# A Fourier mixer over half of the token frequencies, mirrored by a sum and a difference

## What is computed

```python
FOURIER_GROUPS = 4
def fourier_mixer(x, w_out):
    B, S, D = x.shape
    xg = x.astype(jnp.float32).reshape(B, S, FOURIER_GROUPS, D // FOURIER_GROUPS)
    y = jnp.fft.fft2(xg, axes=(1, 3), norm='ortho').real.reshape(B, S, D)
    return y.astype(x.dtype) @ w_out
...
        x = layer_norm(DEEPNORM_ALPHA * x + mix, ln1_gain[layer], ln1_bias[layer])
        ffn = hierarchical_moe_2(x, router_coarse_w[layer], router_coarse_b[layer], router_fine_w[layer],
                               router_fine_b[layer], expert_w_gate[layer], expert_w_up[layer],
                               expert_w_down[layer])
        x = layer_norm(DEEPNORM_ALPHA * x + ffn, ln2_gain[layer], ln2_bias[layer])
```

## Time and profile before

| | us |
|---|---|
| median of 3 runs | 2004.66 |
| lowest and highest run | 2002.22, 2005.18 |
| profiled execution | 2002.44 |
| its span | 2000.5 |
| its mean granted TensorE clock | 0.951 of full |
| Fourier stage in it, first matmul to the first of the next stage | 1451.55 to 1482.64 |

### The profile page before, as it was taken

How to read it: one execution, slowest core, us unless ns; L and a number is a source line. 1 busy time by engine, 2 the same in 40 slices (tenths; PEclk the granted TensorE clock), 3 DMA queues, 4 the chain that set the end, 5 groups by cost and what they waited for, 6 DMA issues and landing times. The chain is left out here.

```text
span 2000.5 us, 20692 instructions
## 1 busy us (share of the span) xinstructions
PE 1785.5 (89%) x8544; PEld 952.9 (48%) x8544; DVE 674.3 (34%) x1347; ACT 427.7 (21%) x713; POOL 83.4 (4%) x66
## 2 busy tenths in 40 slices
PE   7999897895799999799799999899597999998995
PEld 6884454695455555456434443333254344442331
DVE  3657333446223334443412222122303122221223
ACT  2321224352222221222211111111112111111110
POOL 0000001311100000120100000000001000000000
PEclk9999998797899999899799999999897999999998
DMA  5345320004669996432999999999793999999995
GB/s 194 127 162 178 123 88 4 0 1 194 243 249 398 403 419 266 144 155 73 384 423 423 423 423 423 423 424 423 299 375 143 424 423 423 423 423 424 423 423 232
DMA packets 100017, 581.49 MB, mean 291 GB/s; under 512 B 23947, under 2 KB 26251, under 8 KB 34893
## 3 DMA queue, kind: packets, MB, share of 16 engines
q1 hardware_dynamic: 87997, 577.81, 70.8%
q10 hardware_dynamic: 11920, 2.26, 0.6%
HBM read 577.39 MB, written 2.62 MB: 290 GB/s over the span
## 5 line engine op out<-in xcount | busy, mean ns | idle before, releaser
L1717 PE MATMUL up_ps_l<-pool,hT 128*64 128x512 f32 x640 | 143.5, 597 | 13.4 <-DMA pool<-in_expert_w_up 13.4
L1717 PE MATMUL gate_ps_l<-pool,hT 128*64 128x512 f32 x640 | 141.4, 593 | 6.6 <-DMA pool<-in_expert_w_gate 5.3
L446 PE MATMUL proj_ps<-pool,hT 128*128 128x512 f32 x320 | 140.2, 598 | 5.6 <-DVE pool L684 5.6
L1740 PE MATMUL y_ps_l<-pool,hidden_l 128*64 128x512 f32 x640 | 142.6, 596 | 2.3 <-ACT hidden_l L1803 1.4
L1870 DVE SCALAR_TENSOR_TENSOR y_low_l<-y_ps_l,slot_gate_l,y_high_l 128x512 fp32r<-128x512 f32 x64 | 47.1, 751 | 251.2 <-ACT y_high_l L1813 251.2
L438 PE MATMUL proj_ps<-hT,pool 128*128 128x256 f32 x512 | 111.9, 380 | 0.0
L1860 DVE TENSOR_TENSOR hidden_l<-hidden_l,up_ps_l 128x512 f32<-128x512 f32 x32 | 22.0, 688 | 245.2 <-PE up_ps_l L1717 245.2
L438 PEld LDWEIGHTS proj_ps<-hT,pool 128*128 128x128 f32 x512 | 96.9, 190 | 14.8 <-issue 1.8
L446 PEld LDWEIGHTS proj_ps<-pool,hT 128*128 128x128 f32 x320 | 61.4, 192 | 81.3 <-issue 74.7
L1717 PEld LDWEIGHTS gate_ps_l<-pool,hT 128*64 128x64 f32 x640 | 45.5, 137 | 98.4 <-issue 87.6
L1717 PEld LDWEIGHTS up_ps_l<-pool,hT 128*64 128x64 f32 x640 | 43.6, 137 | 99.4 <-issue 77.8
(11 more groups left out here) (503 smaller groups left out, 2682.0 us busy)
## 6 DMA issues: line engine op xcount, KB each, us to landing
pool<-in_expert_w_gate SPq DMA_DIRECT2D x40, 2048.0 KB, 32.4
pool<-in_expert_w_up SPq DMA_DIRECT2D x40, 2048.0 KB, 30.2
pool<-in_expert_w_down SPq DMA_DIRECT2D x40, 2048.0 KB, 32.1
pool<-in_w_in_blocks SPq DMA_DIRECT2D x18, 2048.0 KB, 7.7
pool<-in_moe_w_gate SPq DMA_DIRECT2D x12, 2048.0 KB, 12.6
pool<-in_moe_w_up SPq DMA_DIRECT2D x12, 2048.0 KB, 12.0
pool<-in_moe_w_down SPq DMA_DIRECT2D x12, 2048.0 KB, 11.6
gate_room<-in_expert_w_gate SPq DMA_DIRECT2D x12, 2048.0 KB, 29.9
```

The source lines that it names most:

```text
L446: last = mm(pp[:, n % 2, j * W:(j + 1) * W], k.hT[:, c, j * P:(j + 1) * P], wbuf[n % 2][:, c, :], start=(c == 0), stop=(c == KC - 1))
L1717: last = mm(out[e * CAP:(e + 1) * CAP, 0:H], xg(part * r + c)[:, at:at + CAP], ex.weights(i, e, c), start=(part + c == 0), stop=(part == e ...
L1740: last = mm(Y[e * CAP:(e + 1) * CAP, n], hidT[:, part * r + c, e * CAP:(e + 1) * CAP], ex.weights(i, e, c)[:, n * W:(n + 1) * W], start=(p ...
```

## The change

The table now has three parts of 256 columns for each token half: cosines of frequencies 0 to 128 beside sines of 1 to 127, then all cosines, then all sines, 768 KB in place of 512 KB. The first product takes only the first part, so its matmuls are 256 columns wide and not 512. The second keeps the cosine and the sine contributions apart: for each output chunk two matmuls of 129 columns sum the cosine part and two of 127 columns the sine part, into neighbouring columns of one bank. ScalarE copies once per chunk after the first product (L2479 and L2480 become one) and once after the second, now to a region `uv` with the scale 1/T. VectorE gets three instructions for each chunk: the difference u - v is token frequencies 1 to 127, the sum u + v is frequencies 255 down to 129, written in mirrored order, and frequencies 0 and 128 are copied.

```diff
--- before.py
+++ after.py
@@ -98,8 +98,9 @@
 
     t = np.arange(T)
     ang = 2 * np.pi * ((t[:, None] * t[None, :]) % T) / T
-    both = np.stack([np.cos(ang), np.sin(ang)], 1).astype(np.float32)
-    return np.ascontiguousarray(both.reshape(NJ, P, 2, T).transpose(1, 0, 2, 3))
+    c, s = np.cos(ang), np.sin(ang)
+    rows = np.concatenate([c[:, 0:P + 1], s[:, 1:P], c, s], 1).astype(np.float32)
+    return np.ascontiguousarray(rows.reshape(NJ, P, 3 * T).transpose(1, 0, 2))
 
 
 ROPE_N = 2 * (64 + 32) * NJ
@@ -2441,13 +2442,16 @@
 
 def stage_fourier(k, ahead):
 
     nc = k.nc
-    s_a, s_ao, s_b = (k.sem(f"dft_{n}") for n in ("rows_product", "rows_out", "columns_product"))
+    s_a, s_ao, s_b, s_bo = (k.sem(f"dft_{n}") for n in ("rows_product", "rows_out", "columns_product", "columns_out"))
     scope = ExitStack()
     k.scope = scope
     with scope:
-        a = k.carve(k.gate_room, CHUNK, [P, KC, 2, T])
+        a = k.carve(k.gate_room, CHUNK, [P, KC, T])
+        uv = k.carve(k.gate_room, CHUNK + KC * T, [P, KC, T])
         ps = [k.ps(f"dft_ps{b}", [P, 2, T]) for b in range(8)]
+        cos, sin = slice(0, P + 1), slice(P + 1, T)
         with nc.Block() as block:
             @block.sync
             def _(sp):
@@ -2455,32 +2459,40 @@
 
             @block.tensor
             def _(pe):
+                mm = nc.tensor.matmul
                 pe.wait_ge(k.s_dft, 16)
                 for c in range(KC):
                     for j in range(NJ):
-                        last = nc.tensor.matmul(ps[c][:], k.x[:, j, c * P:(c + 1) * P], k.dft[:, j],
-                                                start=(j == 0), stop=(j == NJ - 1))
+                        last = mm(ps[c][:, 0], k.x[:, j, c * P:(c + 1) * P], k.dft[:, j, 0:T],
+                                  start=(j == 0), stop=(j == NJ - 1))
                     last.then_inc(s_a, 1)
                 for g in range(KC // 2):
-                    pe.wait_ge(s_ao, 4 * (g + 1))
+                    pe.wait_ge(s_ao, 2 * (g + 1))
                     for o in range(2):
-                        n = 0
-                        for f in range(2):
+                        for f, part in ((1, cos), (2, sin)):
                             for q in range(2):
-                                last = nc.tensor.matmul(ps[2 * g + o][:, 0, :], k.dft[:, q, f, o * P:(o + 1) * P],
-                                                        a[:, 2 * g + q, f, :], start=(n == 0), stop=(n == 3))
-                                n += 1
+                                last = mm(ps[2 * g + o][:, 0, part], k.dft[:, q, f * T + o * P:f * T + (o + 1) * P],
+                                          a[:, 2 * g + q, part], start=(q == 0), stop=(q == 1))
                         last.then_inc(s_b, 1)
 
             @block.scalar
             def _(act):
                 for c in range(KC):
                     act.wait_ge(s_a, c + 1)
-                    nc.scalar.activation(a[:, c, 0], ps[c][:, 0], ACT.Copy).then_inc(s_ao, 1)
-                    nc.scalar.activation(a[:, c, 1], ps[c][:, 1], ACT.Copy, scale=-1.0).then_inc(s_ao, 1)
+                    nc.scalar.activation(a[:, c], ps[c][:, 0], ACT.Copy).then_inc(s_ao, 1)
                 for c in range(KC):
                     act.wait_ge(s_b, c + 1)
-                    nc.scalar.activation(k.hT[:, c, :], ps[c][:, 0], ACT.Copy, scale=1.0 / T)
+                    nc.scalar.activation(uv[:, c], ps[c][:, 0], ACT.Copy, scale=1.0 / T).then_inc(s_bo, 1)
+
+            @block.vector
+            def _(dve):
+                tt = nc.vector.tensor_tensor
+                for c in range(KC):
+                    dve.wait_ge(s_bo, c + 1)
+                    u, v = uv[:, c, 1:P], uv[:, c, sin]
+                    tt(k.hT[:, c, 1:P], u, v, ALU.subtract)
+                    tt(k.hT[:, c, T - 1:P:-1], u, v, ALU.add)
+                    nc.vector.tensor_copy(k.hT[:, c, 0:T:P], uv[:, c, 0:P + 1:P])
     k.scope = k.ctx
 
 
@@ -2557,7 +2569,7 @@
             k.ctx = k.scope = outer
         k.gate_room = k.sb("gate_room", [P, 2 * CHUNK])
         split_rows("l")
-        k.dft = k.carve(k.gate_room, 0, [P, NJ, 2, T])
+        k.dft = k.carve(k.gate_room, 0, [P, NJ, 3 * T])
         for n in range(2):
             ex[1 + n].ring(k.gate_room, 2)
             ex[1 + n].ring(k.store, 2)
```

## The result

The changed kernel takes **1990.72 us** (median of 4 runs, 1989.95 to 1991.04), the kernel before, in runs on the same chip, 2004.45 (4 runs, 2002.22 to 2005.18): a ratio of 0.9933, 95% interval 0.9916 to 0.995. That is 13.7 us less by the medians. What of this scatter belongs to the change is a question in itself, taken up after the rows.

The account below looks back on a forecast made before the run. TensorE was taken to bound the Fourier stage, which lies on the path to the first expert and its train of transfers. -13.5 + 0.7 + 0.7 = -12.1 us, put on the median 2004.66: 1992.5 us, range 1989 to 1995.5, with rivals (a) and (b) 1988.8 to 1997.5.

Parts of the forecast that it names:

- The train: Expert-weight transfers from the first expert to the end, 418 us at 421 GB/s, claimed to move as a whole.
- The case in which transfers eat the gain: Rival: weights bound the kernel from 1442 to the end, so a shorter stage only lengthens a wait; 2004.7 us, chance 0.04.
- The rest: DMA standstill ahead of the first expert, ring full: 21 us by which the last loads could land later at no cost.
- the rule that each us is worth 0.5: First product: each us the clock rises earlier or later than 5.2 us after the start changes the saving by 0.5 us.
- +-0.8: First product: allowance in us around the 6.9 us saving for when the clock rises.
- rival (a): Second product: odd widths or the offset of 129 are slow on TensorE; 1995.8 or 1999.2 us, chance 0.09.
- Tail: End of the Fourier stage: VectorE's work on the last chunk lies on the path, +0.7 us.
- rival (b): Second product: VectorE becomes the bound, with a slow mirrored sum; +3.5 us, 1996.0 us, chance 0.05.
- The late bias: Norm after the Fourier stage: `bias_l` lands behind expert chunks, making `turn(0)` wait about +0.7 us (0 to 2.8).
- the landing: Arrival of `bias_l` for the norm after the Fourier stage, forecast at about 1488.4 (1487.3 to 1490.6).
- rival (d): Fourier stage and output product: shorter matmuls leave the clock low, making the kernel slower, up to 2023 us; chance 0.03.

Follow-up runs that it names:

- warm-ups: Changed kernel plus 28 or 15 unused matmuls on TensorE during the norm ahead of the Fourier stage: 1991.6 us with 28, 1991.13 with 15.
- the repeat at 1994.38: The changed kernel measured again without further change, beside 11 runs of the kernel before (2002.7 us): 1994.38 us, ratio 0.9957.
- the halves alone: Kernel before with only the narrow second product and VectorE's sums: 1996.29 us; or with only the first product's cosine half, sines left out: 1994.26 us.
- both kernels with 15 warm-ups: Changed kernel plus 15 unused matmuls during the norm ahead of the stage: 1991.13 us; the same with four expert chunks issued late: 1986.69 us.

## Why the prediction was right, point by point

- **What bounds the kernel: right.** From the first expert on, all fourteen profiles take 459.6 to 461.0 us, whatever the stretch ahead took (88.06 to 102.35). The train is rigid, and it moves by what the path ahead of it saves, as long as the ring fills in time. The case in which transfers eat the gain did not come. The rest was less than the 21 us read from the earlier trace rows: in the kernel before the last load landed at 1523.9 and the first expert began at 1540.6, 16.7 us later. Nothing here came near that.
- **First product: right, a little undersized.** -7.4 us against -6.9, since the clock rose after 4.0 us and not 5.2; the rule that each us is worth 0.5 held (9.5 - 0.6 = 8.9, measured 8.98). The rise scatters, so the product takes 8.62 to 9.46 in seven profiles without warm-ups, inside the +-0.8.
- **Second product: right.** 0.111 us for odd widths and an offset of 129; rival (a) is dead. The nearest rows, 64 and 128 columns in the same type, told the price. The Trainium skill's 81 ns (TensorE: Matmul & The Clock Gate, section Back-to-back issue gap) does not hold for these float32 pairs, which follow one another by 0.111 us: the product takes 7.1 us and not the 5.2 estimated from that figure, and the measurement decides. That the weight load sets the 0.111 is inferred from 64 to 129 columns all taking it; no run changed the load.
- **ScalarE and VectorE: right.** Tail 0.62 against 0.7; VectorE idles 0.32 us before each chunk, so rival (b) is dead. A mirrored float32 write costs what a plain one does. That is what the Trainium skill's rule in SBUF — State Buffer, section Door 1: The DMA port swizzle (why `[64,N]` ≈ `[32,N]`), led one to expect; the traces agree with 0.28 and 0.29 us.
- **The larger table: right.** Alone it gives a ratio of 1.0 (0.9988 to 1.0012). Its load took 1.1 us longer and not 0.6, and landed 5.9 us before the stage began.
- **The late bias: the mechanism right, the term mis-sized.** The sum had +0.7 us (0 to 2.8); measured are +1.8, +2.1 and +2.1. The failing step is the landing: it was put at 1488.4, 1.6 us before the old 1490.0. Counted from t0, the issue came 12.9 us earlier (44.70 to 31.84), and the landing, by the old row and the new wait's end, only 0.4 us earlier (51.7 to 51.3), since the bytes ahead of it in the queue set it. Behind it is a misread row: the fall to 228 GB/s at 1484 was taken for the end of the chunks, but the last chunk of the kernel before landed at 1487.4. Counted from t0 the last chunk was forecast at 46.4 and landed at 48.5, 2.1 us later; from it to the bias 3.7 us were forecast and 2.8 measured, so that the two errors partly cancel and 1.2 us remain. The moment at which the norm wanted it was right to 0.1 us (48.7 forecast, 48.6 measured). And the sum held nothing for the clock that can fall in the pause which the wait makes.
- **The clock: right for the rise, incomplete.** It rose in the shorter stream, and rival (d) did not come. (The two rises of the earlier trace rows were read from the durations of matmuls; by the granted clock they came at 559.05 and 992.55, 4.0 and 6.1 us after their starts.) That it could fall in the output product was not in the list.
- **The total.** The terms gave -12.1 for a profiled execution, which differed by -11.8; of this -1.6 is the earlier t0. By the stretch the change is worth 10.1 to 11.0 us, 1.1 to 2.0 less than forecast: better products (0.5), a dearer bias (1.1 to 1.4, once 0.9 more behind it), and some tenths of scatter. The 1992.5 us lay 1.8 above the measured median; part of that nearness is luck, as the repeat at 1994.38 shows.

Open is what sets the scatter of t0 (it lies in stages that no kernel here changed), and why the clock fell in `out(1, 1)` after idle times of 1.89 and 2.36 us but not after 1.63 and 1.96, although all of these but the 2.36 are of the same kernel. The failing step of the bias and the two parts of its price are shown; that the fall belongs to the pause is only suggested, since no run made the pause at will.

## What to carry to other kernels

When a stage on the path gets shorter, list the small loads that are issued at its end: behind a saturated queue they landed when the bytes ahead of them were through, however early they were issued, and issuing the large loads behind them cost nothing here, since the later train had rest to give. Half of the columns halved a float32 matmul record only down to 0.111 us, the pace that 64, 127, 128 and 129 columns share. Where single executions scatter as widely as the gain, measure from a fixed instruction ahead of the change to one behind it, and look for the term that doesn't add up between the halves alone and together.

## What was unexpected of the hardware

- **The clock fell after short pauses, and with a delay.** TensorE's granted clock went from 1.00 to 0.50 some 0.7 us into the first product after 2.73 and 2.76 us of idle time (both kernels with 15 warm-ups), and in `out(1, 1)`, 1.4 and 1.2 us after work had begun again, after 1.89 and 2.36 us (8.73 us in place of 7.03). After 1.10, 1.63 and 1.96 us it did not. So a pause can be paid for by the work behind it, and warm-up matmuls that leave one are worth little.
- **A small issue can block SyncE for 14 us.** The issue of `router_w_l` took 14.18 us with four expert chunks ahead of it in the queue and 0.67 us with the chunks behind it. Here nobody waited for what stood behind it.
- **A stage's first matmul can come late though nothing holds it:** the warm-ups, which wait for nothing, began 3.7 to 4.1 us after t0 in four profiles, with the idle time before them put down to issue. What holds them is open.
